# Where a column order is undone: in the split of the weights, or in the reads of the accumulation banks

## The reference, cut to what matters

```python
def first_block(...):                     # fox mixer, then a convolutional feed-forward
    a = rms_norm(h, mix_norm)
    q, k, v, f_logit = split(a @ fox_w_in)          # 2048 x (3*2048 + 16)
    ...                                             # 16 heads, forget gates, causal softmax
    h = h + mixed @ fox_w_out                       # 2048 x 2048
    up = rms_norm(h, ffn_norm) @ ffn_w_up           # 2048 x 11264, causal convolution, silu(gate) * value
    h = h + gated @ ffn_w_down                      # 5632 x 2048
def second_block(...):                    # hgrn2 scan and band attention, then a squared-relu feed-forward
    z = rms_norm_2(h) @ w_in                        # 2048 x 11264: 22 chunks of 512 columns
    merged = gate_a * (y_a @ w_branch_a) + gate_b * (y_b @ w_branch_b)
    h = h + merged @ w_out
    h = h + square(relu(rms_norm_2(h) @ w_up)) @ w_down   # 2048 x 8192, 8192 x 2048
    return rms_norm_2(h, norm_final_w)
```

## Time and profile before

| | |
|---|---|
| three runs | 2477.94, 2482.05, 2483.34 us; median 2482.05 |
| profiled execution | 2480.14 us, of which the span 2478.3 us |
| granted TensorE clock, mean | 0.994 |
| PE busy | 2424.9 us (98%), 11468 matmuls |
| DVE busy | 1883.7 us (76%) |
| ACT busy | 1709.0 us (69%) |
| POOL busy | 223.2 us (9%) |
| DMA | 545.79 MB, mean 220 GB/s |

### The profile page before, as it was taken

How to read it: one execution, slowest core, us unless ns; L and a number is a source line. 1 busy time by engine, 2 the same in 40 slices (tenths; PEclk the granted TensorE clock), 3 DMA queues, 4 the chain that set the end, 5 groups by cost and what they waited for, 6 DMA issues and landing times. The chain is left out here.

```text
span 2478.3 us, 32506 instructions
## 1 busy us (share of the span) xinstructions
PE 2424.9 (98%) x11468; PEld 2117.6 (85%) x11468; DVE 1883.7 (76%) x1831; ACT 1709.0 (69%) x1617; POOL 223.2 (9%) x365
## 2 busy tenths in 40 slices
PE   8999999999999999999999999999999999999997
PEld 7888888888888888887988888888888888888886
DVE  6677767888888888886888666577677777777776
ACT  7666668877777777775465667776766666666665
POOL 0122201100000000000010100000110000000000
PEclk9999999999999999999999999999999999999999
DMA  7877768887788788756566767677777777777775
GB/s 228 262 210 214 207 181 252 246 237 238 235 237 236 236 236 235 215 179 204 184 198 188 237 179 214 176 221 239 245 231 226 230 227 227 227 227 229 231 225 160
DMA packets 270391, 545.79 MB, mean 220 GB/s; under 512 B 22011, under 2 KB 23395, under 8 KB 270179
## 3 DMA queue, kind: packets, MB, share of 16 engines
q1 hardware_dynamic: 244064, 469.82, 62.6%
q0 software_dynamic: 22192, 70.28, 10.1%
q10 hardware_dynamic: 4051, 4.59, 0.6%
HBM read 508.93 MB, written 35.68 MB: 220 GB/s over the span
## 5 line engine op out<-in xcount | busy, mean ns | idle before, releaser
L897 ACT ACTIVATE w_hi<-raw 128x1024 fp32r<-128x1024 f32 x887 | 1373.8, 1567 | 547.9 <-PE acc L498 385.8
L1408 DVE TENSOR_TENSOR w_lo<-raw,w_hi 128x1024 fp32r<-128x1024 f32 x887 | 1327.0, 1508 | 496.4 <-ACT w_hi L897 490.3
L496 PE MATMUL acc<-w_hi,A_hi 128*128 128x512 f32 x1932 | 743.6, 385 | 6.1 <-ACT scratch L910 3.5
L497 PE MATMUL acc<-w_lo,A_hi 128*128 128x512 f32 x1932 | 733.1, 379 | 0.0
L498 PE MATMUL acc<-w_hi,A_lo 128*128 128x512 f32 x1932 | 732.9, 379 | 0.0
L496 PEld LDWEIGHTS acc<-w_hi,A_hi 128*128 128x128 f32 x1932 | 365.9, 189 | 59.8 <-DVE w_lo L1408 4.6
L498 PEld LDWEIGHTS acc<-w_hi,A_lo 128*128 128x128 f32 x1932 | 365.9, 189 | 51.6
L497 PEld LDWEIGHTS acc<-w_lo,A_hi 128*128 128x128 f32 x1932 | 366.0, 189 | 50.0
L496 PE MATMUL acc<-w_hi,C_hi 128*128 128x512 f32 x800 | 305.2, 381 | 6.3 <-DVE resid L1455 4.6
L496 PE MATMUL acc<-w_hi,B_hi 128*128 128x512 f32 x800 | 305.7, 382 | 3.1 <-DVE w_lo L1408 2.2
L497 PE MATMUL acc<-w_lo,C_hi 128*128 128x512 f32 x800 | 304.5, 381 | 0.0
(11 more groups left out here) (208 smaller groups left out, 1312.3 us busy)
## 6 DMA issues: line engine op xcount, KB each, us to landing
raw<-in_up SPq DMA_DIRECT2D x304, 512.0 KB, 4.5
raw<-in_w SPq DMA_DIRECT2D x271, 512.0 KB, 4.5
raw<-in_down SPq DMA_DIRECT2D x216, 512.0 KB, 4.8
raw<-in_wo SPq DMA_DIRECT2D x64, 512.0 KB, 5.2
turn_rows<-scratch POOLq DMA_DIRECT2D x23, 512.0 KB, 3.1
scratch<-turn_rows POOLq DMA_DIRECT2D x92, 128.0 KB, 5.2
up_rows<-scratch POOLq DMA_DIRECT2D x21, 512.0 KB, 4.8
scratch<-up_rows POOLq DMA_DIRECT2D x84, 128.0 KB, 5.6
```

Of the source, the lines that this page charges most:

```text
L496: pe.matmul(o, hi[:, kt, ts], wh, start=first and kk == 0, stop=False)
L497: pe.matmul(o, hi[:, kt, ts], wl, start=False, stop=False)
L897: act.activation(by_half(w_hi[:, q % RING, :]), even_odd(raw[:, q % RING, :]), ACT.Copy).then_inc(w_hi_ready, 1)
L1408: dve.tensor_tensor(by_half(w_lo[:, q % RING, :]), even_odd(raw[:, q % RING, :]), f32(by_half(w_hi[:, q % RING, :])), ALU.subtract).then_i ...
```

## The change

The splits read `raw` in order and write in order, so each half of a slot holds 256 neighbouring columns of the matrix. TensorE's instructions are the same, word for word: it still takes the two halves alternately and writes the bank in order. So column n of the first half now stands at place 2n of the bank and column n of the second half at 2n+1. Whoever empties a bank reads it with a step of two, first the even places, then the odd ones (`in_order`), and writes the two halves of the target in order (`halved`).

```diff
-                act.activation(by_half(w_hi[:, q % RING, :]), even_odd(raw[:, q % RING, :]), ACT.Copy).then_inc(w_hi_ready, 1)
+                act.activation(w_hi[:, q % RING, :], raw[:, q % RING, :], ACT.Copy).then_inc(w_hi_ready, 1)
...
-                    to, src = dst[:, t * CW:(t + 1) * CW], acc[:, banks[t], :]
                     if blocks:
-                        to, src = by_block(dst, t), src.rearrange("p (j b q) -> p j b q", j=JT, b=4)
-                    m = act.activation(to, src, func, scale=scale[:, t:t + 1])
+                        m = evacuate_blocks(dst, t, banks[t], scale)
+                    else:
+                        m = act.activation(halved(dst[:, t * CW:(t + 1) * CW]), in_order(acc[:, banks[t], :]), func,
+                                           scale=scale[:, t:t + 1])
...
+            def evacuate_blocks(dst, t, bank, scale, func=ACT.Copy):
+
+                for h in range(2):
+                    src = in_order(acc[:, bank, :])[:, h, :].rearrange("p (j b q) -> p j b q", j=JT // 2, b=4)
+                    m = act.activation(by_block(dst, t)[:, h * JT // 2:(h + 1) * JT // 2], src, func, scale=scale[:, t:t + 1])
+                return m
...
-                dve.tensor_tensor(by_half(w_lo[:, q % RING, :]), even_odd(raw[:, q % RING, :]),
-                                  f32(by_half(w_hi[:, q % RING, :])), ALU.subtract).then_inc(w_lo_ready, 1)
+                dve.tensor_tensor(w_lo[:, q % RING, :], raw[:, q % RING, :], f32(w_hi[:, q % RING, :]),
+                                  ALU.subtract).then_inc(w_lo_ready, 1)
...
-                v = resid[:, :, c * CW:(c + 1) * CW]
-                dve.tensor_tensor(v, v, acc[:, banks[0]:banks[1] + 1, :], ALU.add).then_inc(done, 1)
+                v = resid[:, :, c * CW:(c + 1) * CW].rearrange("p t (h n) -> p t h n", h=2)
+                dve.tensor_tensor(v, v, acc[:, banks[0]:banks[1] + 1, :].rearrange("p t (n h) -> p t h n", h=2),
+                                  ALU.add).then_inc(done, 1)
```

More of the change, by code:

```diff
@@ L373, in in_tokens @@
             return v.rearrange("p k (t a q) -> p (k t) a q", t=TT, a=4)
[L375 to L381, removed]
         def in_turn(w):
@@ L389, in columns, with in_order, halved @@
             return o.rearrange("p (n h) -> p n h", h=2)
+        def in_order(o):
+            return o.rearrange("p (n h) -> p h n", h=2)
+        def halved(v):
+            return v.rearrange("p (h n) -> p h n", h=2)
         @block.sync
@@ L975, in early_split @@
                 v = slice(kk * CW, (kk + 1) * CW)
-                return act.activation(by_half(w_hi[:, 0, v]), even_odd(raw[:, 0, v]), ACT.Copy)
+                return act.activation(w_hi[:, 0, v], raw[:, 0, v], ACT.Copy)
             act.wait_ge(w_early, 16)
@@ L1172, in ups1 @@
                         for t in range(TT):
-                            m = act.activation(by_block(up_q, t), acc[:, BK[c][t], :].rearrange("p (j b q) -> p j b q", j=JT, b=4),
-                                               ACT.Copy, scale=rstd[:, t:t + 1])
+                            m = evacuate_blocks(up_q, t, BK[c][t], rstd)
                         m.then_inc(up1_out, 1)
@@ L1234, in keep_z2 @@
                         for t in range(TT):
[L1235 to L1238, removed]
+                            for h in range(2):
+                                for u in range(2):
+                                    dst = v_pad[:, t, 4 * h:4 * (h + 1), :].rearrange("p (j u) d -> p j u d", u=2)
+                                    src = in_order(acc[:, banks[t], :])[:, h, :].rearrange("p (j u d) -> p j u d", u=2, d=AT_D)
+                                    m = act.activation(dst[:, :, u, u * AT_D:(u + 1) * AT_D], src[:, :, u, :], ACT.Copy,
+                                                       scale=rstd[:, t:t + 1])
                         m.then_inc(z2_out, 1)
@@ L1346, in ups2 @@
                 for t in range(TT):
-                    m = act.activation(by_block(block_q, t), acc[:, BK[3 if first else 0][t], :].rearrange("p (j b q) -> p j b q", j=JT, b=4),
-                                       ACT.Relu, scale=rstd[:, t:t + 1])
+                    m = evacuate_blocks(block_q, t, BK[3 if first else 0][t], rstd, ACT.Relu)
                 m.then_inc(up2_out, 1)
@@ L1490, in early_split @@
                 dve.wait_ge((w0_hi, w_hi_ready)[kk], 1)
-                return dve.tensor_tensor(by_half(w_lo[:, 0, v]), even_odd(raw[:, 0, v]), f32(by_half(w_hi[:, 0, v])), ALU.subtract)
+                return dve.tensor_tensor(w_lo[:, 0, v], raw[:, 0, v], f32(w_hi[:, 0, v]), ALU.subtract)
             early_split(0).then_inc(w0_lo, 1)
@@ L1864, in _ @@
                         dve.wait_ge(half_block, BY_BLOCK.index(TN_MERGE + n - 1) + 1)
-                    g3 = unit(GATE_U[n + NCH * k]).rearrange("p (t c) -> p t c", t=TT)
-                    dve.tensor_tensor((stage_q, stage_k)[k].rearrange("p (t c) -> p t c", t=TT), g3,
-                                      acc[:, 2 * k:2 * k + 2, :], ALU.mult).then_inc(merge_read, 1)
+                    g3 = unit(GATE_U[n + NCH * k]).rearrange("p (t h n) -> p t h n", t=TT, h=2)
+                    dve.tensor_tensor((stage_q, stage_k)[k].rearrange("p (t h n) -> p t h n", t=TT, h=2), g3,
+                                      acc[:, 2 * k:2 * k + 2, :].rearrange("p t (n h) -> p t h n", h=2),
+                                      ALU.mult).then_inc(merge_read, 1)
                     if k == 1:
@@ L1928, in add_tile @@
                 dve.wait_ge(tile_done, 2 * t + c - 1)
-                v = resid[:, t, c * CW:(c + 1) * CW]
-                dve.tensor_tensor(v, v, acc[:, D2_LAST[c][t], :], ALU.add).then_inc(last_added, 1)
+                v = halved(resid[:, t, c * CW:(c + 1) * CW])
+                dve.tensor_tensor(v, v, in_order(acc[:, D2_LAST[c][t], :]), ALU.add).then_inc(last_added, 1)
             def gain_tile(t):
```

## The result

The changed kernel takes 2445.65 us (median of 4 runs, 2442.02 to 2451.70), the kernel before 2482.70 in the same comparison (2477.94 to 2484.87). The ratio is 0.9856, with an interval of 0.9831 to 0.9881: 36 us less by the ratio, 37 by the medians. The forecast was 2471, with a range of 2462 to 2479, so the direction was right and the size three times too small (four times against the sum of 8.9 us). The profiled execution of the changed kernel is the slowest of its four, 2451.70 us with a span of 2449.9, so its trace explains 28 of the 37 us.

A forecast was written before the change was run, and what follows sets the result against it. TensorE, busy 98% of the span, was taken as the bound, so only its waits counted: 11.5 us gained, less 2.3 for bank reads and 0.3 for doubled instructions, took 2480.1 to 2471.2, said as 2471, range 2462 to 2479.

The forecast's parts named there:

- the sum of 8.9 us: Predicted net saving: 11.5 us from shorter waits, less 2.3 for bank reads and 0.3 for doubled instructions.
- what bounds the kernel: TensorE, busy 98% of the span; ACT and DVE work counts only where TensorE waits, and is hidden in feed-forward loops.
- the length of the splits: ACT's split falls from 1567 ns to 1.06 us, DVE's from 1508 ns to 1.21 us, 887 times.
- the bank reads: Emptying banks with a step of two costs 0.25 ns an element, 2.3 us over 9,200 elements on the path.
- The lower bound: For bank reads with a step of two: no cost, as unloaded in SBUF.
- the waits, one by one: TensorE's waits, each shortened by splits ahead of it, 11.5 us in sum before bank reads are charged.
- The four hand-overs: Hand-overs of v (L910, 4.4 us of waits): 0.35 us less each, 1.3 us with the shorter ones.
- `w_lo` waits: Eight TensorE waits for `w_lo` (4.8 + 0.8 us): 0.5 to 0.8 us less each, 3.6 us in all.
- The end of the first feed-forward: Wait for the adds there (4.6 us): about 1.75 us less through both engines, 0.25 for an earlier trip, 2.0 together.
- Rival 1: Shorter waits, as at 1058 us, also keep the clock at its high level: 2465 us, chance 0.17.
- Rival 2: Splits wait for loads or paths end with trips, landing no sooner; savings 11.5 become 5: 2477 us, chance 0.14.
- Rivals 3, 4 and 5: Dear bank reads, 2477 us, 0.10; splits unchanged, ring writes slow, 2483, 0.04; bank reads hold up TensorE's writes, 2489, 0.07.

The follow-up runs named there:

- e8: Kernel before, with splits reading in order only inside the bodies of the two feed-forward loops: 2482.07 us, ratio 1.0004.
- e9: Kernel before, with splits reading in order everywhere except in the two feed-forward loop bodies: 2445.09 us, ratio 0.9862.
- e7: Kernel before, splits still with a step of two, but TensorE reads the weights in order of memory: 2549.97 us.
- e1: Kernel before, with only the splits on ACT and DVE reading in order and banks read as before: 2445.43 us, ratio 0.9863.
- e11: Kernel before, with every weight load after the first four cut to one of its two row tiles: 2449.34 us, ratio 0.9872.
- e13: Changed kernel, with every weight load issued one slot's DVE split later than the ring needs, same bytes: 2512.23 us, ratio 1.0129.

## Why the prediction was right or wrong

**Right: what bounds the kernel.** TensorE's pace did not move, and e8 and e9 show that the loops hid their part of the change.

**Right: the length of the splits.** 1.06 and 1.21 were forecast, 1.056 and 1.222 measured. That the pattern and not the ring was slow is shown by e7, where the splits write the same ring with the same step. The cause given, running matmuls, was too wide: it takes TensorE's alternating read.

**Wrong, but small: the bank reads.** 0.25 ns an element, 2.3 us, was charged; 682 and 1216 ns say 0. The lower bound held, and e1 confirms it in the whole time, to within its spread. The Trainium skill's lines of 8 bytes (PSUM — Partial Sum Buffer, Specifications), read as a rule for whoever reads a bank and with the 0.65 cycle an element of its Vector Engine (DVE) Microarchitecture Reference, section 5.2, would have cost an estimated 6.3 us; the rows show nothing of it.

**Wrong: the waits, one by one.** This is the step that failed. It priced each wait by the one or two splits directly ahead of it, and came to 11.5 us. The medians show 37 us in its place, and the runs show a loop in place of one or two splits: a shorter split issues the next load sooner, which lands sooner. The four hand-overs show what was left out; 0.35 us was forecast for each, and 1.0 to 1.6 us came, because the wait vanished. SP around the last hand-over before (ACT stands in the earlier trace rows); the first of these five loads is the one that ACT's split waits for:

```profile
296.01 8.27 SPq L401 DMA_DIRECT2D raw<-in_wo  x5
```

and SP, with the load for the same slot, and ACT in the same place after:

```profile
282.54 0.37 SPq L401 DMA_DIRECT2D raw<-in_wo  x1
...
288.00 1.06 ACT L897 ACTIVATE w_hi<-raw 128x1024 fp32r<-128x1024 f32 x1 [1.76 <-DMA raw<-in_wo]
289.07 0.69 ACT L910 ACTIVATE scratch<-acc,small 128x512 f32<-128x512 f32 x1
290.37 0.69 ACT L910 ACTIVATE scratch<-acc,small 128x512 f32<-128x512 f32 x1 [0.61 <-PE acc L498]
```

Before, the split in front of the evacuation had waited 2.39 us for its load and began 0.8 us before TensorE's last matmul of the pass (which starts at 301.87 us); now it begins 1.95 us before it (289.95). It still waits for its load, but the load is issued 7.4 us before that matmul, where it was 5.9, since a shorter DVE split was done, behind a shorter ACT split, and it lands 1.2 us sooner relative to TensorE (0.6, 2.1 and 1.5 at the other three). The 0.35 us of its own shortening come on top. At the four hand-overs the split began 0.7, 0.7, 0.2 and 0.8 us before the last matmul; now 1.3, 2.1, 1.7 and 2.0. The same loop, load, ACT's split, DVE's split, next load, runs through the whole kernel; that each turn passes its saving on to the next is argued from this, not measured turn by turn. That landings matter is shown by e11 with the splits left long, and by e13, which delays them. How much of the 37 us goes this way, and how much is the queues' own shortening, is not shown for the whole kernel.

**Where it was mis-sized.** The fox mixer was priced at some 3.5 us (hand-overs 1.3, L604 0.8, its share of the `w_lo` waits) and gave 16.4. Besides 5.1 at the hand-overs, 3.4 came at its end, with the low clock behind L604, and the rest in many steps of 0.2 to 1.1 us around the heads, most of which have no row or share one with others. The 3.4 us are mostly the luck of the profiled execution of the kernel before, not the change: e8, the same program up to there, waited 0.7 us at L604 in place of 1.9 and had no low clock behind it, which alone gave it 2.5 us. Its stretch for the 0.91 of the earlier trace rows:

```profile
300.00:320.00 20.00, 18.33 (x86) 15.29 (x85) 10.96 (x22) 13.98 (x22) 0.00 (x0) 1.00 0.78 237
```

The rows of waits are a floor of what TensorE loses, not the sum of it. The earlier trace rows shows eight of the fifteen rows of that view, 28.7 of 39.8 us (the largest left out is the first wait of all, for the inputs, 5.6 us, which stayed at 5.2). And a wait is counted from the modelled end of a matmul, 0.16 us after the next one could have started, so each is too short by that and the shortest are not there. The end of the first feed-forward was priced at 2.0 us and gave 4.5, of which 2.9 is the low clock that did not return. The prediction took the wait before it for the longest; the longest that the change could touch is the one of 5.4 us at the scan, with a low clock behind it as well, which stayed.

**The rivals.** Rival 1 (the clock comes back) was true in part and was priced only on top of too small a sum: before the final norm the low clock cost 8.5 us in the trace before, 5.1 in the one after and 3.4 in e1's. Rival 2 (loads do not land sooner) was the opposite of what happened; the sentence against it, that a load moves by 0.8 us too, was the missing term, and it was not put into the sum. Rivals 3, 4 and 5 are out: bank reads cheap, splits short, pace unchanged.

**What the trace does not hold.** The traces are 28 us apart and the medians 37. Of the 9 us, 6 are missing because the changed kernel's profiled execution is the slowest of four that differ by 10 us, and 3 because that of the kernel before was faster than its median. e1's profiled execution (2445.49 us) is at the changed kernel's median and shows where such 6 us can lie: 1.7 are low clock (the changed kernel's trace has two stretches of it before the final norm, of 6.8 and 3.4 us at 1.2 GHz), and 1.2 to 1.5 each are longer waits at L744, at L1880 and for `w_lo`. The trace of e9 (2441.75 us) has no low clock before the final norm. Also open is how the 36 us divide between queues and landings: both lie in one loop, and e11 moved the trips as well.

## What to carry to other kernels

When an operation in a producer ring gets shorter, ask what it releases: if the next load is issued at its end, the saving is passed round the ring and appears at the places where stages meet, here in far more than the one or two instances in front of a wait. Price such a change by how much earlier the load lands relative to the consumer, and take the list of waits as a lower bound of what can be won. And put a permutation where few reads undo it, from a memory that does not mind: here bank reads in place of 887 pairs of splits.

## What the runs showed of the hardware

TensorE read fp32r weights of 512 columns fastest when it took two runs 256 words apart in turn: 215.8 ns a matmul; in order it took 226.7, with a step of two 451, all at 2.4 GHz. ACT and DVE paid for the fast pattern: their reads with a step of two went from 1132 and 1221 ns (TensorE in order) to 1567 and 1508 (TensorE alternating), while reads in order took 1056 and 1222 beside it. Reads of PSUM with a step of two cost ACT and DVE nothing (682 for 680 ns, 1216 for 1210).
